# Feed-forward gate and up with the weight blocks held in TensorE and x streamed, so that the gated products come out turned

## The chip, the cores and the metric

The kernel runs on one core of one Trainium2 chip. A core has TensorE (matmuls; PE in the profile, its loads of the stationary operand PEld), VectorE (DVE), ScalarE (ACT), GpSimd (POOL), SyncE (SP, which issues the weight transfers here) and 16 DMA engines. The metric is device microseconds of one execution, less is better. Three runs of the kernel before gave 1437.35 us as their median (1436.28 to 1438.09).

## The reference

x has 256 tokens of width 1024, float32. Two attention blocks come first, then four feed-forward parts with a short convolution and a gated delta rule between them. Only the feed-forward part is changed:

```
def rms_norm_2(x, g):
    xf = x.astype(jnp.float32)
    y = xf * lax.rsqrt(jnp.mean(xf * xf, axis=-1, keepdims=True) + RMS_EPS)
    return (y * g.astype(jnp.float32)).astype(x.dtype)

def swiglu(x, w_gate_up, w_down):
    gate, up = jnp.split(x @ w_gate_up, 2, axis=-1)
    return (jax.nn.silu(gate) * up) @ w_down

        ff = swiglu(rms_norm_2(h, g[0]), ffn_w_gate_up[i, 0], ffn_w_down[i, 0])
        h = h + 0.5 * rms_norm_2(ff, g[1])
```

w_gate_up is 1024 x 5632, w_down 2816 x 1024. In each of the two layers swiglu runs before and after the mixer: four times in all.

## The kernel before, in words

Every large matmul is made of three: each operand is kept as a rounded part and the rest (`x_hi`, `x_lo`, `w_hi`, `w_lo`, all float32r), and hi*hi, hi*lo and lo*hi are summed in PSUM. Weights come in units of 2048 columns per partition (1 MB) through a ring of 4 buffers: SP issues two transfers into `raw`, ACT rounds (`split_hi`, L209), DVE forms the rest (`split_lo`, L227), TensorE uses the unit (`Walk.unit`) and counts it in `unit_used`, which frees the buffer for the load of four units later. `w_hi` and `w_lo` start a unit every 8192 bytes of a partition; `x_hi` and `x_lo` hold eight blocks of 256 columns (1024 bytes each).

A feed-forward part has 11 steps (j = 0 to 10) of 256 hidden columns. A step takes two gate-and-up units (`gate_up(j, 0)` and `gate_up(j, 1)`, each half of the 1024 input rows; 256 gate and 256 up columns side by side) and one down unit (`down`). TensorE works through them in an order written out in `Ffn.pe`: gate-up of step j, then down of step j-1, then `turn(j)`. In a unit TensorE holds a 128x128 block of x (tokens across) and streams 512 weight columns: 24 matmuls. So gate and up come out with tokens across the partitions. The banks of PSUM alternate by step: A for step 0, then G for odd and M for even ones; down sums in the four A banks.

After the second gate-up unit of a step DVE scales by the token's `r` (the norm's reciprocal root, one number per partition here) and clamps (`clamp`, L704), ACT forms the sigmoid in three operations (`sigmoid`, L669 to L671), DVE makes the product `h` (`gate`, L711 and L713), TensorE turns it with four 128x128 transposes (`turn`, L623) into the PSUM bank that gate and up have left, ACT rounds that into `hT_hi` (`hid_hi`, L677), DVE forms `hT_lo` (`hid_lo`, L722), and the down unit takes both as its held operand. The last two down units run interleaved in `last_units`.

Besides these, `Walk.turned_unit` (L280 to L282) is used by the delta-rule part alone: it holds 32-column blocks of weights and streams x's 256 columns. Units of the attention blocks that carry the chunk "gr" stream 272 columns.

Each engine runs its instructions in the order of the code (`Ffn.pe`, `Ffn.dve`, `Ffn.act`, `Ffn.sp`), with semaphores between them.

Of the kernel before, what the change touches and what calls it, by code (L numbers as in the profile page):

```python
# [172 lines left out]
class Walk:  # L173
# [112 lines left out]

    def first_units(self, pre, banks):
# [264 lines left out]
class Ffn:  # L552


    def __init__(self, net, name, w_gu, w_dn, pre_g, post_row, before, brow_free):
# [8 lines left out]
        self.h_turned = net.shared_sem("ffn_h_turned", self.steps)  # L564
# [42 lines left out]
    def turn_bank(self, j):  # L607
        return self.net.M[0] if j == 0 else self.banks(j)[0]
# [8 lines left out]
    def turn(self, w, j):  # L617
        net, pe = self.net, w.eng
        pe.wait_ge(*self.hidden(j + 1))
        bank = self.turn_bank(j)  # L620
        for kk in range(2):
            for tt in range(TT):
                mm = pe.transpose(bank[:, kk * T + tt * P:kk * T + (tt + 1) * P],  # L623
# [8 lines left out]
    def pe(self, w):  # L632
# [40 lines left out]
    def hid_hi(self, w, j):  # L673
        act = w.eng
        act.wait_ge(*self.h_turned(j + 1))
        at = 2 * (j % 2)
        act.activation(self.hT_hi[:, at:at + 2, :], self.turn_bank(j)[:, :], ACT.Copy).then_inc(self.h_hi.sem, 1)  # L677

    def act(self, w):
# [9 lines left out]
        for j in range(1, self.steps):  # L689
            w.split_hi()  # L690
            self.hid_hi(w, j - 1)
# [4 lines left out]
        self.hid_hi(w, self.steps - 1)  # L696
        self.post.act(w)


    def clamp(self, w, j):  # L700
        net, dve = self.net, w.eng
        dve.wait_ge(net.unit_used, self.unit_end["g", j, 1])
        for tt in range(TT):
            ins = dve.tensor_scalar(self.z[:, tt, :], self.banks(j)[tt][:, 0:256], net.r[:, tt:tt + 1], CLAMP,  # L704
                                    ALU.mult, ALU.max)
        ins.then_inc(self.clamped.sem, 1)

# [2361 lines left out]
```

## Time and profile before

| | |
|---|---|
| median of 3 runs | 1437.35 us |
| the profiled execution | 1436.43 us, its span 1434.7 us |
| mean granted clock of TensorE | 0.998 of full speed |
| TensorE matmuls busy | 1412.5 us (98%) |
| weight loads busy | 1159.0 us (81%) |
| VectorE, ScalarE, GpSimd busy | 999.7, 836.4, 67.8 us |
| read from HBM | 235.07 MB, 165 GB/s over the span |

The profiled execution took 1436.43 us of device time, of which the span from the first to the last instruction is 1434.7 us. Matmuls are pipelined: the duration that a row shows is that from start to end of one, and the next one starts long before that end, so the pace of a stretch is read from the starts of its first and last row, not from durations.

### The profile page before, as it was taken

The numbers are of one execution on the slowest core, as the hardware profiler recorded it, in microseconds if no ns is written. First come the engines' busy times: TensorE is split into PE (matmuls) and PEld (weight loads), VectorE is DVE, ScalarE is ACT, GpSimd is POOL, SyncE is SP. The second block draws the span as 40 slices with busy tenths as digits, with TensorE's granted clock in tenths as the row PEclk, the third lists the DMA queues.
The fourth block names the chain that finished last, engine by engine and source line by source line (L and its number), as shares of the span: only waits on it lengthen the run. The fifth ranks groups of instructions, "written<-read, shape, count | busy, mean of one in ns | idle before, by whom it ended". The sixth has DMA issues, their size and how long they took to land.

```text
span 1434.7 us, 20210 instructions
## 1 busy us (share of the span) xinstructions
PE 1412.5 (98%) x8003; PEld 1159.0 (81%) x8003; DVE 999.7 (70%) x1381; ACT 836.4 (58%) x1250; POOL 67.8 (5%) x163
## 2 busy tenths in 40 slices
PE   7999999999999999999999999999999999999998
PEld 6888888888888787788887888887778888788886
DVE  5878788876555766665557656667989876865555
ACT  6657574745454554554445555457888886554444
POOL 8000000000000000000000000001030300000000
PEclk9999999999999999999999999999999999999999
DMA  7543453345556555555655555555453432566562
GB/s 231 166 138 94 158 178 125 110 148 189 192 177 199 180 191 177 172 195 177 192 189 176 192 195 185 181 171 179 142 162 108 119 121 99 175 193 194 177 198 95
DMA packets 168286, 238.24 MB, mean 166 GB/s; under 512 B 21554, under 2 KB 114640, under 8 KB 168192
## 3 DMA queue, kind: packets, MB, share of 16 engines
q1 hardware_dynamic: 166496, 233.57, 50.2%
q0 software_dynamic: 1632, 3.35, 0.8%
q8 instruction: 64, 1.05, 0.3%
q14 instruction: 30, 0.25, 0.1%
q10 hardware_dynamic: 64, 0.02, 0.0%
HBM read 235.07 MB, written 1.84 MB: 165 GB/s over the span
## 4 chain that ended last, share of the span: by engine, by line
PE 93%; DVE 3%; ACT 2%; DMA 1%; issue 1%; SPq 0%; DVEq 0%; ACTq 0%
PE A L245 17%; PE A L246 16%; PE A L247 16%; PE M L245 5%; PE G L245 5%; PE M L247 5%; PE G L247 5%; PE G L246 5%; PE M L246 5%; PE A L1282 1%; PE G L1203 1%; PE G L1250 1%; DMA raw<-in_ffn_w_gate_up 1%; PE M L623 1%; DVE tmp L414 1%; PE M L1260 1%
## 5 line engine op out<-in xcount | busy, mean ns | idle before, releaser
L227 DVE TENSOR_TENSOR w_lo<-raw,w_hi 128x1024 fp32r<-128x1024 f32 (+2 forms) x296 | 506.1, 1731 | 167.8 <-ACT w_hi L209 167.2
L209 ACT ACTIVATE w_hi<-raw 128x1024 fp32r<-128x1024 f32 (+2 forms) x296 | 426.9, 1462 | 161.2 <-DMA raw<-in_ffn_w_gate_up 132.7
L245 PE MATMUL A<-w_hi,x_hi 128*128 128x512 f32 (+1 forms) x640 | 259.3, 405 | 3.6 <-DVE x_lo L419 0.7
L247 PE MATMUL A<-w_hi,x_lo 128*128 128x512 f32 (+1 forms) x640 | 247.5, 387 | 0.0
L246 PE MATMUL A<-w_lo,x_hi 128*128 128x512 f32 (+1 forms) x640 | 247.0, 386 | 0.0
L245 PEld LDWEIGHTS A<-w_hi,x_hi 128*128 128x128 f32 x640 | 120.7, 189 | 33.7 <-DVE x_lo L419 6.6
L247 PEld LDWEIGHTS A<-w_hi,x_lo 128*128 128x128 f32 x640 | 120.4, 188 | 25.3
L245 PE MATMUL A<-w_hi,ffn_ffn_hT_hi 128*128 128x512 f32 x352 | 138.7, 394 | 0.0
L669 ACT ACTIVATE ffn_ffn_e<-ffn_ffn_z 128x512 f32<-128x512 f32 x44 | 27.8, 632 | 190.2 <-DVE ffn_ffn_z L704 190.2
L246 PE MATMUL A<-w_lo,ffn_ffn_hT_hi 128*128 128x512 f32 x352 | 138.4, 393 | 0.0
L246 PEld LDWEIGHTS A<-w_lo,x_hi 128*128 128x128 f32 x640 | 120.9, 189 | 21.0 <-issue 0.7
L247 PE MATMUL A<-w_hi,ffn_ffn_hT_lo 128*128 128x512 f32 x352 | 137.2, 390 | 0.0
L245 PE MATMUL M<-w_hi,x_hi 128*128 128x512 f32 x320 | 126.6, 396 | 0.0
L245 PE MATMUL G<-w_hi,x_hi 128*128 128x512 f32 x320 | 126.5, 395 | 0.0
L247 PE MATMUL M<-w_hi,x_lo 128*128 128x512 f32 x320 | 124.8, 390 | 0.0
L247 PE MATMUL G<-w_hi,x_lo 128*128 128x512 f32 x320 | 124.8, 390 | 0.0
L246 PE MATMUL G<-w_lo,x_hi 128*128 128x512 f32 x320 | 124.6, 389 | 0.0
L246 PE MATMUL M<-w_lo,x_hi 128*128 128x512 f32 x320 | 124.5, 389 | 0.0
L711 DVE TENSOR_TENSOR ffn_ffn_gs<-ffn_ffn_z,ffn_ffn_e 128x512 f32<-128x512 f32 x44 | 30.4, 692 | 81.0 <-ACT ffn_ffn_e L671 81.0
L247 PEld LDWEIGHTS A<-w_hi,ffn_ffn_hT_lo 128*128 128x128 f32 x352 | 66.1, 188 | 14.9
L245 PEld LDWEIGHTS A<-w_hi,ffn_ffn_hT_hi 128*128 128x128 f32 x352 | 66.1, 188 | 14.7
L246 PEld LDWEIGHTS A<-w_lo,ffn_ffn_hT_hi 128*128 128x128 f32 x352 | 66.2, 188 | 13.1
(388 smaller groups left out, 2033.0 us busy)
## 6 DMA issues: line engine op xcount, KB each, us to landing
raw<-in_ffn_w_gate_up SPq DMA_DIRECT2D x176, 512.0 KB, 4.8
raw<-in_ffn_w_down SPq DMA_DIRECT2D x88, 512.0 KB, 4.2
raw<-in_w_in SPq DMA_DIRECT2D x48, 512.0 KB, 4.4
raw<-in_gdn_w_in SPq DMA_DIRECT2D x48, 512.0 KB, 4.6
raw<-in_sc_w_in SPq DMA_DIRECT2D x24, 512.0 KB, 4.7
raw<-in_w_out SPq DMA_DIRECT2D x16, 512.0 KB, 4.3
raw<-in_gdn_w_out SPq DMA_DIRECT2D x16, 512.0 KB, 4.1
raw<-in_w_mem_kv SPq DMA_DIRECT2D x8, 512.0 KB, 5.8
```

What stands on the lines that cost most here:

```text
L209: ins = act.activation(net.w_hi[:, v % RING, part], net.raw[:, v % RING, part], ACT.Copy)
L227: ins = dve.tensor_tensor(net.w_lo[:, v % RING, part], net.raw[:, v % RING, part], net.w_hi[:, v % RING, part].bitcast(F32), ALU.subtract)
L245: pe.matmul(out, xh, hi[:, k, c, :], start=start and k == 0, stop=False)
L246: pe.matmul(out, xh, lo[:, k, c, :], start=False, stop=False)
L247: mm = pe.matmul(out, xl, hi[:, k, c, :], start=False, stop=stop and k == nk - 1)
L414: dve.tensor_tensor(self.y(n), self.banks[n][:, :].rearrange("p (k t) -> p k t", k=4), self.g[:, 4 * h:4 * h + 4].unsqueeze(2).to_broadcas ...
L623: mm = pe.transpose(bank[:, kk * T + tt * P:kk * T + (tt + 1) * P], self.h[:, tt, kk * P:(kk + 1) * P], net.ident[:, :])
L669: w.chain(act.activation(self.e[:, :, :], self.z[:, :, :], ACT.Exp, scale=-1.0))
L711: w.chain(dve.tensor_tensor(self.gs[:, :, :], self.z[:, :, :], self.e[:, :, :], ALU.mult))
L1203: mm = pe.matmul(bank[:, n * P + t * 64:n * P + (t + 1) * 64], self.KE[rows, 1 + lev, tok], right, start=True, stop=True, tile_position=(D ...
L1250: mm = pe.matmul(bank[:, at:at + keys], qT[rows, pair, tt * P:(tt + 1) * P], kT[rows, pair, 0:keys], start=True, stop=True, tile_position= ...
L1260: mm = pe.transpose(bank[:, b * P:(b + 1) * P], self.Pb[:, i % 3, b * P:(b + 1) * P], ident[:, :])
```

## The change

Steps 1 to 10 of each feed-forward part form gate and up the other way round: the new `turned_blocks` holds a 128x128 block of weights and streams the 256 columns of x, so a unit is four column blocks times four row blocks times three: 48 matmuls of 256 columns in place of 24 of 512. The first bank gets the gate's two blocks, the second the up's. They come out turned, hidden columns across the partitions, as the down unit wants them. The transposes of steps 1 to 10 are gone, `hid_hi` and `hid_lo` read `h` in SBUF, and TensorE waits for `hidden` of step j-2 before it writes that step's banks. Step 0 stays as it was.

Since tokens now lie along the free dimension, r must be a row repeated on all partitions: DVE spreads each token's r over 128 columns (`r_cols`), two matmuls against the identity turn it, and ACT copies it to `rT` once in each part. `clamp` and `gate` become five DVE operations over 512 elements instead of five over 256 or 512.

```
+    def turned_blocks(self, x_hi, x_lo, k0, nk, banks, start, stop):
+
+        net, u, pe = self.net, self.u, self.eng
+        n = nk * 4 * P
...
+        hi = net.w_hi[:, u % RING, 0:n].rearrange("p (k n) -> p k n", k=nk)
+        lo = net.w_lo[:, u % RING, 0:n].rearrange("p (k n) -> p k n", k=nk)
+        pe.wait_ge(net.w_lo_ready, u + 1)
+        for c in range(4):
+            out, cols = banks[c // 2][:, c % 2 * T:(c % 2 + 1) * T], slice(c * P, (c + 1) * P)
+            for k in range(nk):
+                pe.matmul(out, hi[:, k, cols], x_hi[:, k0 + k, :], start=start and c % 2 == 0 and k == 0, stop=False)
+                pe.matmul(out, hi[:, k, cols], x_lo[:, k0 + k, :], start=False, stop=False)
+                mm = pe.matmul(out, lo[:, k, cols], x_hi[:, k0 + k, :], start=False,
+                               stop=stop and c % 2 == 1 and k == nk - 1)
+        mm.then_inc(net.unit_used, 1)
+        self.u += 1
...
     def gate_up(self, w, j, kh):
         net = self.net
-        if kh == 0 and j >= 2:
-            w.eng.wait_ge(*self.h_lo(j - 1))
-        b0, b1 = self.banks(j)
-        w.unit(net.x_hi, net.x_lo, 4 * kh, 4, 512, [[b0], [b1]], kh == 0, kh == 1)
+        if kh == 0 and j == 2:
+            w.eng.wait_ge(*self.h_lo(1))
+            w.eng.wait_ge(*self.rT_ready(1))
+        elif kh == 0 and j > 2:
+            w.eng.wait_ge(*self.hidden(j - 1))
+        w.turned_blocks(net.x_hi, net.x_lo, 4 * kh, 4, self.banks(j), kh == 0, kh == 1)
+
+    def turn(self, w):
         net, pe = self.net, w.eng
-        pe.wait_ge(*self.hidden(j + 1))
-        bank = self.turn_bank(j)
+        pe.wait_ge(*self.r_spread(1))
+        for tt in range(TT):
+            mm = pe.matmul(net.M[1][:, tt * P:(tt + 1) * P], self.r_cols[:, tt, :], net.ident[:, :],
+                           start=True, stop=True)
+        mm.then_inc(self.r_rows.sem, 1)
+        pe.wait_ge(*self.hidden(1))
...
         self.gate_up(w, 1, 0)
-        self.turn(w, 0)
+        self.turn(w)
         self.gate_up(w, 1, 1)
         self.down(w, 0)
-        self.turn(w, 1)
         last = self.steps - 1
         for j in range(2, last):
             self.gate_up(w, j, 0)
             self.gate_up(w, j, 1)
             if j < last - 1:
                 self.down(w, j - 1)
-                self.turn(w, j)
         self.gate_up(w, last, 0)
-        self.turn(w, last - 1)
         self.gate_up(w, last, 1)
         self.down(w, last - 2)
-        self.turn(w, last)
...
+    def clamp(self, w, j):
+        net, dve = self.net, w.eng
+        r = self.rT[:, :].unsqueeze(1).to_broadcast([P, 2, T])
+        gate, up = (bank[:, :].rearrange("p (k t) -> p k t", k=2) for bank in self.banks(j))
+        if j == 1:
+            dve.wait_ge(*self.rT_ready(1))
+        dve.wait_ge(net.unit_used, self.unit_end["g", j, 1])
+        w.chain(dve.tensor_tensor(self.z[:, :, :], gate, r, ALU.mult))
+        dve.tensor_scalar(self.z[:, :, :], self.z[:, :, :], CLAMP, None, ALU.max).then_inc(self.clamped.sem, 1)
+        w.chain.mark(dve.tensor_tensor(self.gs[:, :, :], up, r, ALU.mult))
+
+    def gate(self, w, j):
+        dve = w.eng
+        w.chain.sync()
+        dve.wait_ge(*self.clamped(j + 1))
+        w.chain(dve.tensor_tensor(self.gs[:, :, :], self.gs[:, :, :], self.z[:, :, :], ALU.mult))
+        dve.wait_ge(*self.gated(j + 1))
+        dve.tensor_tensor(self.h[:, :, :], self.gs[:, :, :], self.e[:, :, :], ALU.mult)\
+           .then_inc(self.hidden.sem, 1)
```

On TensorE, at the border between the down unit of step 0 and the gate-up of step 2 of the first feed-forward part, before the change (a row's last field is the streamed columns as partitions x columns; `h` is the product to be turned):

```order
L246 MATMUL A<-w_lo,ffn_ffn_hT_hi 128x512
L247 MATMUL A<-w_hi,ffn_ffn_hT_lo 128x512
L623 MATMUL G<-ident,ffn_ffn_h 128x128 x4
L245 MATMUL M<-w_hi,x_hi 128x512
L246 MATMUL M<-w_lo,x_hi 128x512
```

Such a group of four transposes stood behind every down unit but the last ones; the gate-up behind it now follows directly. What is left of it in the changed kernel is this one place in each part, between the two gate-up units of step 1, with the two new matmuls that turn r ahead of it:

```order
L300 MATMUL G<-x_hi,w_lo 128x256
L643 MATMUL M<-ident,ffn_ffn_r_cols 128x128 x2
L649 MATMUL M<-ident,ffn_ffn_h 128x128 x4
L298 MATMUL G<-x_hi,w_hi 128x256
L299 MATMUL G<-x_lo,w_hi 128x256
L300 MATMUL G<-x_hi,w_lo 128x256
```

On DVE a middle step before the change, from its clamp to that of the next step (L227 are the rests of weight units):

```order
L704 TENSOR_SCALAR ffn_ffn_z<-M,small 128x256 x2
L711 TENSOR_TENSOR ffn_ffn_gs<-ffn_ffn_z,ffn_ffn_e 128x512
L713 SCALAR_TENSOR_TENSOR ffn_ffn_h<-M,small,ffn_ffn_gs 128x256 x2
L227 TENSOR_TENSOR w_lo<-raw,w_hi 128x2048 x2
L722 TENSOR_TENSOR ffn_ffn_hT_lo<-M,ffn_ffn_hT_hi 128x512
L227 TENSOR_TENSOR w_lo<-raw,w_hi 128x2048
```

and the same stretch now:

```order
L759 TENSOR_TENSOR ffn_ffn_z<-M,ffn_ffn_rT 128x512
L760 TENSOR_SCALAR ffn_ffn_z<-ffn_ffn_z 128x512
L761 TENSOR_TENSOR ffn_ffn_gs<-M,ffn_ffn_rT 128x512
L767 TENSOR_TENSOR ffn_ffn_gs<-ffn_ffn_gs,ffn_ffn_z 128x512
L769 TENSOR_TENSOR ffn_ffn_h<-ffn_ffn_gs,ffn_ffn_e 128x512
L227 TENSOR_TENSOR w_lo<-raw,w_hi 128x2048
L776 TENSOR_TENSOR ffn_ffn_hT_lo<-ffn_ffn_h,ffn_ffn_hT_hi 128x512
L227 TENSOR_TENSOR w_lo<-raw,w_hi 128x2048 x2
```

Here `hT_lo` is formed one weight unit earlier than before, and out of SBUF.

## Rows read from the trace of the kernel before

**Rows 1.** The page: busy time of engines, clock, share of the last-ending chain.

```profile
PE 1412.5 (98%) x8003; PEld 1159.0 (81%) x8003; DVE 999.7 (70%) x1381; ACT 836.4 (58%) x1250; POOL 67.8 (5%) x163
...
PEclk9999999999999999999999999999999999999999
...
PE 93%; DVE 3%; ACT 2%; DMA 1%; issue 1%; SPq 0%; DVEq 0%; ACTq 0%
```

**Rows 2.** Waits of PE, the longest: us in total, times, longest.

```profile
PE M L3046 <- DMA rows<-in_g_pre: 7.4, 1, 7.4
```

**Rows 3.** Timeline of PE, step 2 of the first part: start, us, what.

```profile
372.25 0.60 PE L623 MATMUL G<-ident,ffn_ffn_h 128*128 128x128 f32 x4
372.60 0.48 PE L245 MATMUL M<-w_hi,x_hi 128*128 128x512 f32 x1
...
378.18 0.39 PE L245 MATMUL M<-w_hi,x_hi 128*128 128x512 f32 x1
...
383.62 0.39 PE L245 MATMUL A<-w_hi,ffn_ffn_hT_hi 128*128 128x512 f32 x1
...
389.12 0.60 PE L623 MATMUL M<-ident,ffn_ffn_h 128*128 128x128 f32 x4
389.48 0.48 PE L245 MATMUL G<-w_hi,x_hi 128*128 128x512 f32 x1
```

**Rows 4.** Timeline of PE, 32 weight columns held, x's 256 streamed.

```profile
987.01 0.28 PE L280 MATMUL A<-x_hi,w_hi 128*32 128x256 f32 x1
...
988.60 0.28 PE L282 MATMUL A<-x_lo,w_hi 128*32 128x256 f32 x1
```

**Rows 5.** Timeline of PE, 128x128 blocks of x held, 272 columns streamed.

```profile
178.00 0.29 PE L245 MATMUL A<-w_hi,x_hi 128*128 128x272 f32 x1
...
181.03 0.40 PE L245 MATMUL A<-w_hi,x_hi 128*128 128x512 f32 x1
```

**Rows 6.** Timeline of PE, eight plain float32 matmuls of 128 columns.

```profile
1146.42 1.05 PE L2478 MATMUL M<-gdn_gd_S,gdn_gd_MT 128*128 128x128 f32 x8
```

**Rows 7.** Weight loads by form: shape, count, busy us, mean ns.

```profile
L245 PEld LDWEIGHTS G<-w_hi,x_hi 128*128 128x128 f32 x320 | 60.1, 188 | 11.9
...
L280 PEld LDWEIGHTS A<-x_hi,w_hi 128*32 128x32 f32 x8 | 0.9, 108 | 1.2 <-ACT gdn_gd_u L2514 1.2
```

**Rows 8.** Groups by form, DVE and ACT: busy us, mean ns, idle before.

```profile
L227 DVE TENSOR_TENSOR w_lo<-raw,w_hi 128x2048 fp32r<-128x2048 f32 x145 | 329.5, 2290 | 149.0 <-ACT w_hi L209 148.9
L711 DVE TENSOR_TENSOR ffn_ffn_gs<-ffn_ffn_z,ffn_ffn_e 128x512 f32<-128x512 f32 x44 | 30.4, 692 | 81.0 <-ACT ffn_ffn_e L671 81.0
L414 DVE TENSOR_TENSOR tmp<-G,cols 128x512 f32<-128x512 f32 x16 | 10.6, 689 | 3.0 <-PE G L361 2.6
L2755 DVE TENSOR_SCALAR gdn_gd_sg<-gdn_gd_t 128x512 f32<-128x512 f32 x16 | 6.7, 427 | 0.1
```

**Rows 9.** Busy time by engine in that step, clock, DMA share, GB/s.

```profile
372.60:389.48 16.88, 16.88 (x80) 13.92 (x78) 9.84 (x10) 7.87 (x8) 0.00 (x0) 1.00 0.59 187
```

**Rows 10.** Timeline of DVE in that step: a weight unit, then the clamp.

```profile
380.85 2.29 DVE L227 TENSOR_TENSOR w_lo<-raw,w_hi 128x2048 fp32r<-128x2048 f32 x1 [4.11 <-ACT w_hi L209]
383.81 0.88 DVE L704 TENSOR_SCALAR ffn_ffn_z<-M,small 128x256 f32<-128x256 f32 x2 [0.67 <-PE M L247]
```

**Rows 11.** Timeline of DVE and PE at the last step of that part.

```profile
479.56 0.88 DVE L704 TENSOR_SCALAR ffn_ffn_z<-M,small 128x256 f32<-128x256 f32 x2 [1.58 <-PE M L247]
...
484.27 2.29 DVE L227 TENSOR_TENSOR w_lo<-raw,w_hi 128x2048 fp32r<-128x2048 f32 x1 [0.20 <-ACT w_hi L209]
486.48 0.68 DVE L722 TENSOR_TENSOR ffn_ffn_hT_lo<-M,ffn_ffn_hT_hi 128x512 fp32r<-128x512 f32 x1
...
485.22 0.48 PE L245 MATMUL A<-w_hi,ffn_ffn_hT_hi 128*128 128x512 f32 x1
```

**Rows 12.** Timeline of DVE and PE around step 0's turn.

```profile
325.60 0.88 DVE L713 SCALAR_TENSOR_TENSOR ffn_ffn_h<-A,small,ffn_ffn_gs 128x256 f32<-128x256 f32 x2
...
327.07 0.60 PE L623 MATMUL M<-ident,ffn_ffn_h 128*128 128x128 f32 x4
```

More of the change, by code:

```diff
@@ L285, in turned_unit @@
             self.u += 1
+    def turned_blocks(self, x_hi, x_lo, k0, nk, banks, start, stop):
+        net, u, pe = self.net, self.u, self.eng
+        n = nk * 4 * P
+        assert net.sizes[u] == n, (u, net.sizes[u], n)
+        hi = net.w_hi[:, u % RING, 0:n].rearrange("p (k n) -> p k n", k=nk)
[10 more added lines that the diff above has]
+        self.u += 1
     def first_units(self, pre, banks):
@@ L563, in __init__ @@
         self.hidden = net.shared_sem("ffn_hidden", self.steps)
-        self.h_turned = net.shared_sem("ffn_h_turned", self.steps)
+        self.h_turned = net.shared_sem("ffn_h_turned", 1)
+        self.r_spread = net.shared_sem("ffn_r_spread", 1)
+        self.r_rows = net.shared_sem("ffn_r_rows", 1)
+        self.rT_ready = net.shared_sem("ffn_rT", 1)
         self.h_hi = net.shared_sem("ffn_h_hi", self.steps)
@@ L582, in tensors @@
         self.h = net.sb("ffn_h", [P, TT, 256])
+        self.r_cols = net.sb("ffn_r_cols", [P, TT, P])
+        self.rT = net.sb("ffn_rT", [P, T])
         self.hT_hi = net.sb("ffn_hT_hi", [P, 4, T], F32R)
@@ L673, in hid_hi @@
     def hid_hi(self, w, j):
[L674 to L677, printed above, removed]
+        act, at = w.eng, 2 * (j % 2)
+        if j == 0:
+            act.wait_ge(*self.h_turned(1))
+            src = self.net.M[0][:, :]
+        else:
+            act.wait_ge(*self.hidden(j + 1))
+            src = self.h[:, :, :]
+        if j >= 2:
+            act.wait_ge(self.net.unit_used, self.unit_end["d", j - 2])
+        act.activation(self.hT_hi[:, at:at + 2, :], src, ACT.Copy).then_inc(self.h_hi.sem, 1)
     def act(self, w):
@@ L690, in act @@
             w.split_hi()
-            self.hid_hi(w, j - 1)
+            if j == 1:
+                act.wait_ge(*self.r_rows(1))
+                act.activation(self.rT[:, :], self.net.M[1][:, 0:T], ACT.Copy).then_inc(self.rT_ready.sem, 1)
+                self.hid_hi(w, 0)
             if j < self.steps - 1:
@@ L695, in act, with first_clamp, first_gate @@
             w.split_hi()
-        self.hid_hi(w, self.steps - 1)
+            self.hid_hi(w, j)
         self.post.act(w)
-    def clamp(self, w, j):
+    def first_clamp(self, w):
         net, dve = self.net, w.eng
-        dve.wait_ge(net.unit_used, self.unit_end["g", j, 1])
+        dve.wait_ge(net.unit_used, self.unit_end["g", 0, 1])
         for tt in range(TT):
-            ins = dve.tensor_scalar(self.z[:, tt, :], self.banks(j)[tt][:, 0:256], net.r[:, tt:tt + 1], CLAMP,
+            ins = dve.tensor_scalar(self.z[:, tt, :], self.banks(0)[tt][:, 0:256], net.r[:, tt:tt + 1], CLAMP,
                                     ALU.mult, ALU.max)
         ins.then_inc(self.clamped.sem, 1)
-    def gate(self, w, j):
+        for tt in range(TT):
+            ins = dve.tensor_scalar(self.r_cols[:, tt, :], net.ident[:, :], 0.0, net.r[:, tt:tt + 1],
+                                    ALU.mult, ALU.add)
+        ins.then_inc(self.r_spread.sem, 1)
+    def first_gate(self, w):
         net, dve = self.net, w.eng
-        dve.wait_ge(*self.gated(j + 1))
+        dve.wait_ge(*self.gated(1))
         w.chain(dve.tensor_tensor(self.gs[:, :, :], self.z[:, :, :], self.e[:, :, :], ALU.mult))
         for tt in range(TT):
-            ins = dve.scalar_tensor_tensor(out=self.h[:, tt, :], in0=self.banks(j)[tt][:, 256:512],
+            ins = dve.scalar_tensor_tensor(out=self.h[:, tt, :], in0=self.banks(0)[tt][:, 256:512],
                                            scalar=net.r[:, tt:tt + 1], in1=self.gs[:, tt, :],
@@ L734, in dve @@
         dve.wait_ge(*self.pre.r_ready(1))
-        self.clamp(w, 0)
+        self.first_clamp(w)
         w.split_lo()
-        self.gate(w, 0)
+        self.first_gate(w)
         for j in range(1, self.steps):
             w.split_lo()
-            self.hid_lo(w, j - 1)
+            if j == 1:
+                self.hid_lo(w, 0)
             if j < self.steps - 1:
@@ L745, in dve @@
             w.split_lo()
-        self.hid_lo(w, self.steps - 1)
+            self.hid_lo(w, j)
         self.post.dve(w)
```

12 lines of the change are left out of this document (5 added, 7 removed).

## The prediction

> **What bounds the kernel now.** I read the page first. TensorE's matmuls are busy 98% of the span, the chain that ended last lies on PE for 93% of it, and the clock's row shows 0.9 or more of full speed in all 40 slices [rows 1]; the step I use below has 1.00 [rows 9], the upper of the two levels, 2.4 GHz. Next the waits: the longest that PE has is 7.4 us at the program's start [rows 2], and none of any feed-forward part is among them. DVE is busy 9.84 us and ACT 7.87 us of a 16.88 us step, the DMA engines 0.59 of it [rows 9]. So the time is the sum of what TensorE issues, and a change is worth what it takes from or adds to that row of starts. The reader should see that busy shares and durations can't tell it: a 512-column matmul shows 0.39 to 0.48 us, yet 24 of them start within 5.44 us. Only starts give the price.
>
> **A step in starts.** In step 2 [rows 3] the second gate-up unit runs from 378.18 to 383.62: 5.44 us for 24 matmuls, 226.7 ns each. The first one, right behind the transposes, runs from 372.60 to 378.18: 5.58 us, 0.14 more for the same work, so a group of transposes also costs a slow restart. The down unit takes 5.50 us (383.62 to 389.12), and the transposes 0.36 us (389.12 to 389.48). 5.58 + 5.44 + 5.50 + 0.36 = 16.88 us.
>
> **Removed.** Ten groups of four transposes in each of four parts. Each is 0.36 us, and the restart behind it 0.14 us: 40 x 0.50 = 20.0 us, all of it on TensorE's row. The transposes waited for `hidden` and had no idle time in front of them, so no more than that is saved. The restart I count whole, since the border between two kinds of fp32r units without transposes between them, 383.62, shows none: the down unit is 5.50 us and the gate-up in front of it 5.44.
>
> **The price of a pair.** This term decides. A gate-up unit was 24 pairs (load of the held block, matmul) of 512 columns and becomes 48 of 256; there are 80 such units, 3840 new pairs. So each nanosecond by which a pair is over or under half of 226.7, which is 113.4, is worth 3.84 us. No row shows this very pair. The nearest:
> - The same streamed operand, x's 256 columns, with blocks of 32 weight columns held, summed into one place of a bank as here: from 987.01 to 988.60 are 14 pairs, 1.59 us, 113.6 ns each [rows 4]. This is again half of the 512-column pace within the rounding, so streaming costs in proportion to columns and no fixed cost per matmul shows.
> - What differs there is the load: 32 columns, 108 ns, against 188 ns for 128 [rows 7]. The difference, 80 ns for 96 columns, is 0.83 ns a column, so that 128 columns should occupy the load path for about 107 ns, an estimate. Eight float32 matmuls of 128 columns with full 128-column loads take 1.05 us with the last one's whole length of about 0.27; the seven gaps are 0.78 us, 111 ns each [rows 6]. A full load fits into 111 ns, then, and 113.4 is more, by 2 ns. This is thin.
> - Blocks of x held, 272 columns streamed: 24 pairs from 178.00 to 181.03, 3.03 us, 126.2 ns each [rows 5]. In proportion 272 columns would be 120.4, so these pay 5.8 ns each. Less 16 columns, that would be 119.5 at 256.
>
> The first and second say 113.4, the third 119.5. I take 113.4. The third row's weight blocks start every 272 columns, 1088 bytes; those of the new code, held and streamed, all start at multiples of 512 bytes from their tiles' starts, as the operands of the gate-up before do, which runs at 226.7 with no such extra. That the starts are the reason is a guess, and the range keeps both ends.
>
> The Trainium skill's page "TensorE: Matmul & The Clock Gate", section "LDWEIGHTS (loading the stationary operand)", has a load take its columns over 1.2 GHz, 107 ns for 128; the trace agrees in its slope [rows 7]. Its section "Back-to-back issue gap" gives a matmul of N columns N/2.4 + 2.5 ns: 109.2 for 256, by which the sum would be 16 us lower than mine. The trace contradicts it at both widths, 226.7 against 215.8 and 113.6 against 109.2.
>
> With 113.4, the 80 units cost 48 x 113.4 = 5.44 us as before: 0.
>
> **Added on TensorE.** Eight matmuls that turn r, two per part, 0.11 us each by the 111 ns gap [rows 6]: 0.9 us. They wait for `r_spread`, formed on DVE right after step 0's clamp, a whole weight unit ahead of the turn. Behind them the remaining turn waits for step 0's `hidden`. It is done at 326.48 and used at 327.07 [rows 12]; the two spreads ahead of it on DVE, 128 columns each and so under 0.43 us each [rows 8], add at most 0.7 with their start, while the turn itself starts 0.2 later for the r matmuls. Cost 0 to 0.1 us a part.
>
> **DVE and ACT.** In a middle step DVE did two scale-and-clamps, one product, two fused products and the rest. Now it has four two-operand products and one rest over 512 elements, 0.69 us each [rows 8], and a clamp of 0.43: 3.9 us, with three weight units of 2.29 us [rows 8] 10.8 us of a step of 16.4. It was 9.84 [rows 9]. That is hidden below 5.6 us of slack, and the wait it sits on has moved: `hT_lo` was needed by a transpose chain and is now needed by the down unit that follows 10.9 us of gate-up. ACT's work is the same but for one copy in a part. If the cover were gone, the 1 us a step would cost 40 us; it would need another 5 us of DVE work.
>
> A place where the slack is small is the last step of a part [rows 11]. `hT_lo` ends at 487.16; `last_units` needs it 12 matmuls, 2.77 us, behind 485.22, at 487.99. The new kernel's TensorE is there 0.5 us sooner (487.49), and the clamp's two dependent operations, 0.69 + 0.43 with a semaphore's way between, take 0.3 longer than the 0.88 before, which delays sigmoid, weight unit and `hT_lo` to 487.46. I count 0.1 us for each part, 0 to 0.4: 0.4 us in all.
>
> The weight stream: a step reads 3 MB at 187 GB/s [rows 9]; 0.5 us less makes it 192. The DVE half of a weight unit ends at 383.14, when the clamp's matmuls end near 383.6 [rows 10], and TensorE wants that unit only after the down unit and the transposes, at 389.48. 6.3 us of slack; losing 0.5 costs nothing.
>
> **Sum**, against the profiled execution's 1436.4: -20.0 + 0 + 0.9 + 0.1 + 0.4 = -18.6, 1417.8 us. The median of the runs shown is 0.9 higher, so 1418.7 against it.
>
> **Rivals.**
> 1. Forecast: the pair costs 112 to 114.5 ns: 1413 to 1423 us. Chance 0.62.
> 2. In between, 114.5 to 117.4 ns: the load, 2 ns short of being the bound, slips out in part. 1423 to 1434 us, 0.12.
> 3. The other side: a 128-column load that runs beside the whole of a short stream disturbs it as in [rows 5], 5.8 ns a pair or more. At 119.5 ns the extra is 6.1 x 3.84 = 23.4 us, 1442 us: slower by 0.3%. Should a pair cost 126.2, it would be 1468. It decides from 118.9 ns on, where 21 us have gone. For it: 272-column pairs have 9 ns more room over the load than the new ones, and yet pay. Against it: [rows 4] and the 512-column units pay nothing. Chance 0.21, of which 0.05 lies within 0.2% of before.
> 4. The page's 109.2 ns: 1403 us; against it stand both paces above. 0.03.
> 5. TensorE's saving is eaten by another wait, the weight stream or DVE's chain ahead of the down unit: steps stay near 16.9 us, 1437 us. Only with 5 us of slack gone on every step; DMA engines busy 0.59. 0.02.
>
> **The numbers.** A measurement of this kernel tells about 0.2%, 2.9 us, from no change. Faster: cases 1, 2 and 4, 0.76 with a little of 2 taken off. Within 0.2%: 0.08, from 3, 5 and the edge of 2. Slower 0.16, all from case 3. The range, 1413.5 to 1438, holds 1, 2, 5 and the near edge of 3; its low end is a pair of 112 ns, the load's own pace.
>
> **What would show it.** In the changed trace, a gate-up unit of 48 starts within 5.44 us (5.74 means rival 3, 5.24 rival 4); a step from clamp to clamp of 16.4 us; no slow restart behind a down unit; loads still 188 ns long; no wait of PE for `h` or `hT_lo` over 0.4 us; 160 fewer transposes. The forecast is wrong if the pair isn't 113.4 ns, and by 3.84 us for each nanosecond; anything else here is under 2 us.

## The result, and the profile after

| | median us | lowest to highest | runs |
|---|---|---|---|
| before | 1437.12 | 1436.28 to 1438.09 | 5 |
| after | 1444.04 | 1441.67 to 1445.86 | 5 |

The ratio is 1.0045 (1.0033 to 1.0057): the change makes the kernel 0.45% slower, 6.9 us. The forecast was 1418.7. The profiled execution took 1441.67 us.

The page of the changed kernel, the rows that answer to [rows 1]:

```profile
PE 1418.3 (99%) x9779; PEld 1243.1 (86%) x9779; DVE 1027.4 (71%) x1389; ACT 835.7 (58%) x1254; POOL 67.9 (5%) x163
...
PEclk9999999999999999999999999999999999999999
...
PE 93%; DVE 2%; ACT 2%; DMA 2%; issue 1%; SPq 0%; DVEq 0%; ACTq 0%
```

The clock is as before, and TensorE is still the chain. Its longest wait is still the one at the start, and no matmul of a feed-forward step stands in the list, neither for `h` nor for `hT_lo`:

```profile
PE M L3099 <- DMA rows<-in_g_pre: 6.7, 1, 6.7
```

So the loss must lie in TensorE's own pace. Step 2 in starts, from the timeline of PE, against [rows 3]:

```profile
370.50 0.28 PE L298 MATMUL M<-x_hi,w_hi 128*128 128x256 f32 x1
...
382.02 0.40 PE L245 MATMUL A<-w_hi,ffn_ffn_hT_hi 128*128 128x512 f32 x1
...
387.53 0.28 PE L298 MATMUL G<-x_hi,w_hi 128*128 128x256 f32 x1
```

A pair is one load of a held block with its matmul. The two gate-up units, 96 pairs, take 382.02 - 370.50 = 11.52 us, 120.0 ns a pair; the down unit 5.51. The step is 17.03 us where it was 16.88 and the forecast had 16.4. The next one is 16.99, so a step costs 0.13 us more on average, 5 us in forty.

Step 0 of that part, where r is turned ahead of `hidden`:

```profile
324.36 0.60 PE L643 MATMUL M<-ident,ffn_ffn_r_cols 128*128 128x128 f32 x4
324.80 0.60 PE L649 MATMUL M<-ident,ffn_ffn_h 128*128 128x128 f32 x4
325.16 0.36 PE L298 MATMUL G<-x_hi,w_hi 128*128 128x256 f32 x1
```

The two r matmuls show as four rows (x4) and take 0.44 us; 1.8 us over four parts.

The step by windows (busy time of PE, PEld, DVE, ACT, POOL, then clock, DMA share and GB/s), against [rows 9], and two loads of a whole block by form, against [rows 7]:

```profile
370.50:387.53 17.03, 17.03 (x122) 16.03 (x120) 10.52 (x10) 7.97 (x8) 0.00 (x0) 1.00 0.56 186
```

```profile
L299 PEld LDWEIGHTS G<-x_lo,w_hi 128*128 128x128 f32 x640 | 122.6, 192 | 0.9
L298 PEld LDWEIGHTS M<-x_hi,w_hi 128*128 128x128 f32 x640 | 121.1, 189 | 0.7
```

DVE has 10.52 us, 0.3 under the estimate; clock and memory traffic are those of before; a load is about as long as it was, 189 to 192 ns against 188. At the last step of the part:

```profile
485.98 0.68 DVE L776 TENSOR_TENSOR ffn_ffn_hT_lo<-ffn_ffn_h,ffn_ffn_hT_hi 128x512 fp32r<-128x512 f32 x1
...
486.83 0.46 PE L245 MATMUL A<-w_hi,ffn_ffn_hT_hi 128*128 128x512 f32 x1
```

`hT_lo` ends at 486.66, just ahead of its matmul; the slip there is under 0.1 us.

### The profile page after: what moved, and what is told of

It reads as the page before. It is cut to its first block, busy times and chain, and to the rows that moved or that the text cites. A ratio compares the mean times of both kernels' runs of the same rounds, so it can differ in the third digit from the quotient of the medians.

```text
span 1439.9 us, 23894 instructions
## 1 busy us (share of the span) xinstructions
PE 1418.3 (99%) x9779; PEld 1243.1 (86%) x9779; DVE 1027.4 (71%) x1389; ACT 835.7 (58%) x1254; POOL 67.9 (5%) x163
## 4 chain that ended last, share of the span: by engine, by line
PE 93%; DVE 2%; ACT 2%; DMA 2%; issue 1%; SPq 0%; DVEq 0%; ACTq 0%
PE A L245 17%; PE A L247 16%; PE A L246 16%; PE M L298 5%; PE M L299 5%; PE M L300 5%; PE G L300 5%; PE G L298 5%; PE G L299 5%; PE A L1335 1%; PE G L1256 1%; PE G L1303 1%; DMA raw<-in_ffn_w_gate_up 1%; DVE tmp L432 1%; PE M L1313 1%
## 5 line engine op out<-in xcount | busy, mean ns | idle before, releaser
L227 DVE TENSOR_TENSOR w_lo<-raw,w_hi 128x1024 fp32r<-128x1024 f32 (+2 forms) x296 | 508.2, 1730 | 190.0 <-ACT w_hi L209 189.0
L298 PE MATMUL M<-x_hi,w_hi 128*128 128x256 f32 x640 | 181.2, 283 | 0.0
L298 PE MATMUL G<-x_hi,w_hi 128*128 128x256 f32 x640 | 181.2, 283 | 0.0
L299 PE MATMUL M<-x_lo,w_hi 128*128 128x256 f32 x640 | 181.2, 283 | 0.0
L300 PE MATMUL M<-x_hi,w_lo 128*128 128x256 f32 x640 | 181.2, 283 | 0.0
L300 PE MATMUL G<-x_hi,w_lo 128*128 128x256 f32 x640 | 181.0, 283 | 0.0
L299 PE MATMUL G<-x_lo,w_hi 128*128 128x256 f32 x640 | 180.9, 283 | 0.0
L299 PEld LDWEIGHTS G<-x_lo,w_hi 128*128 128x128 f32 x640 | 122.6, 192 | 0.9
L298 PEld LDWEIGHTS G<-x_hi,w_hi 128*128 128x128 f32 x640 | 122.6, 192 | 0.8
L300 PEld LDWEIGHTS G<-x_hi,w_lo 128*128 128x128 f32 x640 | 122.6, 192 | 0.0
L298 PEld LDWEIGHTS M<-x_hi,w_hi 128*128 128x128 f32 x640 | 121.1, 189 | 0.7
```

Source lines behind the costliest of these rows:

```text
L227: ins = dve.tensor_tensor(net.w_lo[:, v % RING, part], net.raw[:, v % RING, part], net.w_hi[:, v % RING, part].bitcast(F32), ALU.subtract)
L298: pe.matmul(out, hi[:, k, cols], x_hi[:, k0 + k, :], start=start and c % 2 == 0 and k == 0, stop=False)
L299: pe.matmul(out, hi[:, k, cols], x_lo[:, k0 + k, :], start=False, stop=False)
L300: mm = pe.matmul(out, lo[:, k, cols], x_hi[:, k0 + k, :], start=False, stop=stop and c % 2 == 1 and k == nk - 1)
```

## The experiments

Three theories stood at the outset. A pair costs 120.0 because **the load is the bound** in a short pair; because each float32r (fp32r) matmul has a **fixed cost** (at one column in each cycle of 2.4 GHz, 256 columns are 106.7 ns, 13.3 less than 120.0; 512 are 213.3, 13.4 less than 226.7); or because load and stream **disturb each other**. The later runs ask by what. A time of one execution has no interval, the others have. Some kernels leave products incomplete; they are there for the pace only.

**turnsback.** The changed kernel with the forty groups of transposes put back, their result unused.

```diff
+    def turn_idle(self, w, j):
+        pe = w.eng
+        pe.wait_ge(*self.hidden(j + 1))
+        bank = self.banks(j)[0]
+        for kk in range(2):
+            for tt in range(TT):
+                pe.transpose(bank[:, kk * T + tt * P:kk * T + (tt + 1) * P],
+                             self.h[:, tt, kk * P:(kk + 1) * P], self.net.ident[:, :])
...
                 self.down(w, j - 1)
+                self.turn_idle(w, j)
```

> The changed kernel with the four transposes of steps 1 to 10 put back behind the same down units, their result thrown away (they wait for h and write into a bank that nobody reads until it is overwritten). Theory (the removed part was priced right at 0.36 us plus 0.14 us of slow restart, 0.50 us a time, 40 times): 20 us more than the changed kernel. Rival (the transposes cost only their own 0.36 us, since the restart is slow in some other way with 256-column pairs): 14.4 us more, the unit behind the transposes as long as the others.

```profile
373.84 0.60 PE L645 MATMUL G<-ident,ffn_ffn_h 128*128 128x128 f32 x4
374.20 0.36 PE L298 MATMUL M<-x_hi,w_hi 128*128 128x256 f32 x1
...
385.79 0.39 PE L245 MATMUL A<-w_hi,ffn_ffn_hT_hi 128*128 128x512 f32 x1
```

1461.11 us, ratio 1.0166 (1.0145 to 1.0186), about 17 us over the changed kernel, between the 14.4 and the 20 expected. A group is 0.36 us, and the gate-up behind it 11.59, 0.08 over the 11.51 mean of a step without it: 0.44 x 40 = 17.6. What the change removes is real, then; the loss is made elsewhere.

**split256.** The kernel before, x's blocks held, but each gate-up stream of 512 cut into two of 256.

```diff
+            if halves:
+                for n, (a, b) in enumerate(((0, 256), (256, 512))):
+                    pe.matmul(out[:, a:b], xh, hi[:, k, c, a:b], start=start and k == 0 and n == 0, stop=False)
...
+                continue
             pe.matmul(out, xh, hi[:, k, c, :], start=start and k == 0, stop=False)
```

> The kernel before, with every 512-column matmul of the gate-up of steps 1 to 10 cut in two of 256 on the same held block of x, so that the same products are formed by 3840 more pairs; transposes as before. Theory F (a pair of a 128-column float32r load and a matmul of N columns takes N/2.4 + 13.3 ns): 120.0 ns a pair, 5.76 us a unit, about 25 us more than the kernel before (1462 us in its profiled execution). Theory L (the load alone takes 120 ns, streams cost in proportion to columns): 120 ns too. Rival R (the extra cost comes from weights being held and x streamed, or from where they lie): 113.4 ns a pair and 1437 us.

```profile
371.29 0.48 PE L247 MATMUL M<-w_hi,x_hi 128*128 128x256 f32 x2
...
382.88 0.39 PE L254 MATMUL A<-w_hi,ffn_ffn_hT_hi 128*128 128x512 f32 x1
```

1457.14 us in one execution. 96 pairs in 11.59 us, 120.7 with the slow restart behind the transposes in it. So it is not the swap of operands: 256-column pairs are dear in either role.

**held64, held112, stream128.** The changed kernel with smaller pairs in 10 or 11 of 12: 64 or 112 weight columns held, or 128 tokens streamed.

```diff
-                pe.matmul(out, hi[:, k, cols], x_lo[:, k0 + k, :], ...)
+                some = slice(c * P, c * P + 64)      # held112: 112
+                pe.matmul(out[0:64], hi[:, k, some], x_lo[:, k0 + k, :], ...)
```

```diff
+                pe.matmul(out[:, 0:128], hi[:, k, cols], x_lo[:, k0 + k, 0:128], ...)   # stream128
```

> The changed kernel with only the first 64 of each 128 held weight columns used in 10 of 12 matmuls, so that half of the gate and up products are left incomplete; streams of 256 columns as before. Theory L (load-bound pairs): a load of half the columns is far from the bound, and pairs fall to 113.4 ns. Theory F (a fixed cost a pair, 13.3 ns with 128 held columns and 6.7 with 32): between the two, about 115.6 ns if it grows evenly with held columns. Rival I (a load that runs beside the stream disturbs it, and half the load disturbs half as long): about 116.7 ns.

```profile
369.87 0.28 PE L302 MATMUL M<-x_lo,w_hi 128*64 128x256 f32 x1
...
370.89 0.28 PE L302 MATMUL M<-x_lo,w_hi 128*64 128x256 f32 x1
```

Nine pairs in 1.02 us, 113.3 ns: in this kernel half a load beside 256 columns takes the extra away. Where whole blocks stand between them (2 of 12), the 96 pairs of a step take 11.03 us, 114.9 each. 1424.12 us in one execution. The load-bound theory had told 113.4; the next run decides about it.

> The changed kernel with only the first 128 tokens streamed in 11 of 12 matmuls (half of the products are left incomplete); loads of 128 columns as before. Theory L (a float32r load of 128 columns takes 120 ns whatever is streamed): pairs stay at 120 ns. Theory F (13.3 ns on top of the stream, the load hidden as long as it fits): the stream of 53 + 13 ns is far shorter than the load, and the pair falls to the load's own pace, about 111 ns as with the eight plain float32 matmuls.

```profile
368.78 0.28 PE L299 MATMUL M<-x_hi,w_hi 128*128 128x128 f32 x1
...
369.78 0.33 PE L299 MATMUL M<-x_hi,w_hi 128*128 128x256 f32 x1
```

Nine pairs in 1.00 us, 111 ns, with whole loads. A load that can follow a load every 111 ns is no bound of 120, and that theory falls. 1413.98 us in one execution.

> The changed kernel with 112 of each 128 held weight columns used in 10 of 12 matmuls (part of the products is left incomplete), streams of 256. Theory P: a load of 112 columns beside the stream takes 112/128 of 120, or 105 ns, less than the stream's 113.4, so pairs fall to 113.4. Theory F with a part that grows from 64 to 128 columns: about 118 ns.

```profile
372.58 0.28 PE L299 MATMUL M<-x_hi,w_hi 128*128 128x256 f32 x1
...
383.94 0.40 PE L245 MATMUL A<-w_hi,ffn_ffn_hT_hi 128*128 128x512 f32 x1
```

11.36 us for 96, 118.3 ns (11.30 us in every other step, 117.7), 1436.59 us in one execution: in between. At 256 columns the extra grows with the held columns above 64. A fixed cost per matmul would not: 113.3 with 64 held rules it out as the whole story.

**bstream384, bheld64, bheld64b.** The kernel before with 384 of 512 columns streamed in 10 of 12, and with 64 of 128 tokens held in 10 of 12, or nearly all.

```diff
-            pe.matmul(out, xh, lo[:, k, c, :], start=False, stop=False)
+            pe.matmul(out[:, 0:384], xh, lo[:, k, c, 0:384], ...)          # bstream384
+            pe.matmul(out[0:64, :], xh[:, 0:64], lo[:, k, c, :], ...)     # bheld64, bheld64b
```

> The kernel before, with 384 instead of 512 columns streamed in 10 of 12 matmuls of the gate-up of steps 1 to 10 (part of the products is left incomplete), 128 tokens held. Theory P: 170.0 ns a pair. Theory F: 160 + 13.3 = 173.3 ns.

```profile
364.90 0.34 PE L248 MATMUL M<-w_lo,x_hi 128*128 128x384 f32 x1
...
366.46 0.33 PE L248 MATMUL M<-w_lo,x_hi 128*128 128x384 f32 x1
```

Nine pairs in 1.56 us, 173.3 ns. 120.0, 173.3 and 226.7 lie 53.3 ns apart for 128 columns each, one column in a cycle of 2.4 GHz. With whole blocks held at these places the pace is thus columns over 2.4 GHz plus 13.3 ns at all three widths: the 226.7 from which I took a half had that constant in it once, and two halves have it twice.

> The kernel before, with only 64 of each 128 tokens of x held in 10 of 12 matmuls of the gate-up of steps 1 to 10 (half of the products are left incomplete), streams of 512 weight columns. Theory P (streaming costs 17/16 of N/2.4, and a pair is the longer of this and of a load that is slowed by a stream running beside it): 226.7 ns a pair, no gain. Theory F (a pair is N/2.4 plus a fixed part that goes with the held columns, 6.7 ns up to 64 and 13.3 for 128): 220.0 ns.

> The kernel before, with 64 of 128 tokens held in all but the first and last matmuls of an accumulation (half of the products are left incomplete), streams of 512: long unmixed rows of half loads, which the earlier run with mixed shapes didn't give. Theory F (N/2.4 plus a part that goes with the held columns): 220.0 ns. Theory P (with half loads the stream's cost is 17/16 of N/2.4): 226.7 ns.

The second, from its timeline of PE:

```profile
372.95 0.48 PE L247 MATMUL M<-w_hi,x_hi 128*128 128x512 f32 x1
...
384.07 0.39 PE L247 MATMUL A<-w_hi,ffn_ffn_hT_hi 128*128 128x512 f32 x1
```

11.12 us for 48, 231.7 ns, where the same stretch with whole blocks took 11.02, 229.6 ns [rows 3] (both with the slow restart behind the transposes), and 1440.7 us for each of the two kernels in one execution: slower than with whole blocks. Neither theory had that, and it stays open. That half a load takes the extra away is seen at 256 columns only.

**hpad, hpad_after, allpad.** Was the place in memory the reason? By the sizes of the tensors, one behind the other as the kernels allocate them, the weight tensors and x's two parts start at the same place modulo 1024 bytes, and `hT_hi` 704 bytes behind it. From here on "n bytes off" is this distance from the weights' place. A pad of 320 bytes takes `hT_hi` to it, and `hT_lo`, 4096 bytes behind, with it. hpad does it to the kernel before, hpad_after to the changed one, allpad also to the memory and convolution operands.

```diff
+        net.sb("ffn_pad", [P, 80])        # 320 bytes a partition
         self.hT_hi = net.sb("ffn_hT_hi", [P, 4, T], F32R)
```

> The kernel before, with 320 unused bytes a partition in front of hT_hi, so that hT_hi and hT_lo start at the same multiple of 1024 bytes as x_hi and the weight units do. Theory A (the down unit's 229.1 ns a pair against 226.7 of gate-up come from where its held blocks lie against the streamed ones): the 44 down units fall from 5.50 to 5.44 us, 2.4 us less than before in all (ratio 0.9983). Rival (they come from the PSUM banks changing every six matmuls): no change.

```profile
367.15 0.39 PE L245 MATMUL A<-w_hi,ffn_ffn_hT_hi 128*128 128x512 f32 x1
...
372.60 0.60 PE L624 MATMUL G<-ident,ffn_ffn_h 128*128 128x128 f32 x4
```

The down unit takes 5.45 us, 227.1 ns a pair, where it took 5.50 [rows 3]; 1434.18 us, ratio 0.9982 (0.9971 to 0.9992). No instruction was changed, so the place of the held operand has a price: 2.1 ns a pair.

> The changed kernel with the 320 unused bytes in front of hT_hi that made the down unit of the kernel before faster. If the two are independent: the down unit falls from 5.50 to 5.45 us, 2.3 us less than the changed kernel, about 1441.5 us, still slower than before by 0.3%.

1443.50 us, 1.0041 (1.0028 to 1.0055), gate-up still 11.51 to 11.52 us a step: `hT_hi`'s place alone does not move the 120. The down unit takes 5.46.

> The kernel before with hT_hi, the memory operands mem_hi and the short convolution's y_hi all moved to the same multiple of 1024 bytes as x_hi and the weight units. Theory A: the down units as in the run with hT_hi alone (2.4 us), the memory operands' 234 ns pairs and the convolution's 229 ns pairs fall to 227, another 192 x 7 + 192 x 6 + 96 x 2.3 ns, 2.7 us: 5 us less than before, ratio 0.9965. Rival: only hT gives anything, 0.9982.

A memory unit in allpad, whose 11 pairs from the second on took 2.56 us before:

```profile
296.11 0.39 PE L246 MATMUL A<-w_lo,block_mem_hi 128*128 128x512 f32 x1
...
298.63 0.39 PE L245 MATMUL A<-w_hi,x_hi 128*128 128x512 f32 x1
```

2.52 us here, 229.1 ns instead of 232.7. In the total it does not show beyond hpad: 1434.08 us, 0.9981 (0.9968 to 0.9994), where 0.9965 was expected.

**xpad, xpad_timed.** The changed kernel with x moved by 704 bytes, and `hT` with it. The second is the same kernel, timed.

```diff
+        self.sb("x_pad", [P, 176])        # 704 bytes a partition
         self.x_hi = self.sb("x_hi", [P, KT, T], F32R)
```

> The changed kernel with 704 unused bytes a partition in front of x_hi and x_lo, so that the streamed blocks start at other multiples within 1024 bytes than the held weight blocks. Theory A (where held and streamed blocks start against each other matters for short pairs too): a pair of 256 costs more than 120.0, 2 to 6 ns. Rival (120.0 is the fixed cost alone, and starts matter only to some shapes): 120.0 as it was. In units where x is held and 512 weight columns are streamed, theory A gives 229 ns in place of 226.7.

> The changed kernel with x_hi and x_lo moved by 704 bytes, the same kernel as the look that gave 1430.6 us, now timed. Theory E (the rhythm is fixed by the program, by what each stretch enters with): about 1430 us in every run, ratio 0.9955 to the kernel before. Rival (it is chance from run to run): a median between 1430 and 1446 with a wide spread.

From xpad_timed, the timeline of PE:

```profile
367.12 0.39 PE L246 MATMUL A<-w_hi,ffn_ffn_hT_hi 128*128 128x512 f32 x1
...
372.69 0.28 PE L299 MATMUL M<-x_hi,w_hi 128*128 128x256 f32 x1
...
383.58 0.39 PE L246 MATMUL A<-w_hi,ffn_ffn_hT_hi 128*128 128x512 f32 x1
```

Gate-up takes 10.89 us, 113.4 ns a pair: the forecast's price, with whole loads and the same instructions. The down unit, whose held tensor is now 384 bytes off, pays 5.57 us. 1425.26 us (1423.67 to 1426.57, 6 runs), ratio 0.9920 (0.9906 to 0.9935). xpad had the same pace by step 2, against both of its expectations, and 1430.55 us in one execution, from which the second expectation took its 1430. Three of its feed-forward parts are as long as here (169.9 to 170.1 us in both). The difference lies between the third part and the fourth, 290.8 us against 286.0: there TensorE stood still for 1.4 us twice, and from 1068 to 1072 us its granted clock was 0.57.

The two executions of this one kernel also differ in pace elsewhere. The stretch of [rows 4], 32 weight columns held, whose 14 pairs took 1.59 us in the kernel before, from the timelines of PE in xpad and then in xpad_timed:

```profile
979.76 0.28 PE L281 MATMUL A<-x_hi,w_hi 128*32 128x256 f32 x1
...
981.44 0.28 PE L283 MATMUL A<-x_lo,w_hi 128*32 128x256 f32 x1
```

```profile
979.18 0.28 PE L281 MATMUL A<-x_hi,w_hi 128*32 128x256 f32 x1
...
980.77 0.28 PE L283 MATMUL A<-x_lo,w_hi 128*32 128x256 f32 x1
```

That is 1.68 and 1.59 us, 120.0 and 113.6 ns a pair, at clock 1.00 and with the DMA engines busy throughout in both. The first unit of the first part takes 5.65 us in xpad and 5.46 in xpad_timed, 117.7 and 113.8 ns. So the same instructions at the same addresses can run at two paces, from one execution to the next; and a light load is no guarantee of the fast one. In kernels with x and the weights where the kernel before has them, the same 14 pairs take 113.6 (before, held64), 115.0 (bheld64, stream128) or 115.7 ns (after, turnsback, bstream384).

**bx704, ax704.** x 704 bytes off and `hT` brought to the weights' place, in both kernels, so that operands are swapped at equal placement.

```diff
+        self.sb("x_pad", [P, 176])
         self.x_hi = self.sb("x_hi", [P, KT, T], F32R)
...
+        net.sb("ffn_pad", [P, 160])
         self.hT_hi = net.sb("ffn_hT_hi", [P, 4, T], F32R)
```

> The kernel before with x_hi and x_lo moved by 704 bytes and hT_hi padded so that it starts where the weight units do (modulo 1024). Theory A (place of held against streamed blocks): the pairs that hold x and stream 512 columns cost 229.3 instead of 226.7 ns, down units 5.45 us; 3840 pairs of x more by 2.6 ns, 10 us, and the x units of the other parts by 1 to 2 ns, less 2.4 us for hT: about 1447 us. Rival (the distance matters to 256-column pairs alone): 1435.

```profile
371.25 0.48 PE L246 MATMUL M<-w_hi,x_hi 128*128 128x512 f32 x1
...
382.34 0.39 PE L246 MATMUL A<-w_hi,ffn_ffn_hT_hi 128*128 128x512 f32 x1
```

11.09 us against 11.02 [rows 3]: 512-column pairs lose 1.5 ns by this move, where 2.6 were expected. 1439.58 us, 1.0020 (1.0011 to 1.0029).

> The changed kernel with x moved by 704 bytes, as in the look that gave 1430.6, and hT_hi padded back to the weight units' place. Theory A: 256-column pairs 113.4 ns, down units 5.45 us instead of 5.58 (44 of them, 5.7 us): about 1425 us, ratio 0.992 to the kernel before. Rival (the look was a chance of that run, or the pad of hT_hi moves something else): 1430 or more.

```profile
320.72 0.28 PE L299 MATMUL G<-x_hi,w_hi 128*128 128x256 f32 x1
...
326.18 0.38 PE L645 MATMUL M<-ident,ffn_ffn_r_cols 128*128 128x128 f32 x2
...
371.47 0.28 PE L299 MATMUL M<-x_hi,w_hi 128*128 128x256 f32 x1
...
382.77 0.39 PE L246 MATMUL A<-w_hi,ffn_ffn_hT_hi 128*128 128x512 f32 x1
...
388.21 0.28 PE L299 MATMUL G<-x_hi,w_hi 128*128 128x256 f32 x1
```

A miss, and a telling one. The first unit of the part runs 48 pairs in 5.46 us, 113.8 ns. In step 2 the same kind of pair, at the same placement (modulo 1024), takes 11.30 us for 96, 117.7 ns, behind a down unit of 5.44. It is so in all four parts: the two units of step 1, which no down unit precedes, run fast (the second takes 5.54 with its restart), and every one from step 2 on runs at 117.7 to 117.8, also the last step, which follows a gate-up directly. There are two paces at one placement, and here what ran ahead seems to pick. 1435.06 us, 0.9983 (0.9974 to 0.9992).

**ax64, ax256.** As ax704, x 64 and 256 bytes off.

```diff
+        self.sb("x_pad", [P, 16])         # ax256: 64
...
+        net.sb("ffn_pad", [P, 64])        # ax256: 16
```

> As ax704, with x moved by 64 bytes only. If the load and the stream, which start together, meet in the same piece of memory only when they lie at nearly the same place: 113.4 ns already. If only a large distance frees them: near 120.

```profile
357.81 0.28 PE L299 MATMUL G<-x_hi,w_hi 128*128 128x256 f32 x1
...
369.12 0.40 PE L246 MATMUL A<-w_hi,ffn_ffn_hT_hi 128*128 128x512 f32 x1
```

> As ax704, with x moved by 256 bytes. If the conflict goes by the distance within 512 bytes (704 is 192 there) and grows smoothly: 113 to 117 ns. If what frees the pair is the distance alone being other than 0: 113.4. Units that hold x and stream 512: 229 to 234.

```profile
355.39 0.28 PE L299 MATMUL G<-x_hi,w_hi 128*128 128x256 f32 x1
...
366.91 0.40 PE L246 MATMUL A<-w_hi,ffn_ffn_hT_hi 128*128 128x512 f32 x1
```

11.31 us (117.8 ns) and 11.52 us (120.0 ns); 1442.23 and 1442.89 us in one execution each. Neither is what its expectation had. The first unit of a part, ahead of any down unit, gives the same order without that influence: 5.75 us in the changed kernel and in ax256, 5.65 in ax64, 5.46 in ax704.

**axh320.** x 704 bytes off, and `hT` too: both now sit where `hT` sat in the kernel before.

```diff
+        self.sb("x_pad", [P, 176])
...
+        net.sb("ffn_pad", [P, 80])
```

> As xpad_timed, with hT_hi and hT_lo moved by another 320 bytes, so that they start where x does (modulo 1024). Theory E: the down unit's own pairs change to the 226, 229, 232 ns pattern of x (5.50 us), and the gate-up stretches behind it run at 113.4 or at 117.8 ns, all alike; 1427 us or 1444 us. Rival (hT_hi's place can't reach the gate-up pairs, and ax704 was slow for another reason): 113.4 ns and 1427 us.

```profile
369.80 0.28 PE L299 MATMUL M<-x_hi,w_hi 128*128 128x256 f32 x1
...
380.70 0.39 PE L246 MATMUL A<-w_hi,ffn_ffn_hT_hi 128*128 128x512 f32 x1
...
386.20 0.28 PE L299 MATMUL G<-x_hi,w_hi 128*128 128x256 f32 x1
```

Gate-up 10.90 us, 113.5 ns; down 5.50; a step of 16.40, which is the step the prediction named. The down unit's place does reach the gate-up pairs, then: ax704 differs from this kernel in nothing else. **1421.63 us** (1419.44 to 1423.89, 5 runs), ratio 0.9895 (0.9880 to 0.9910): 1.0% faster than the kernel before and about 1.5% faster than the changed one. Against the kernel before at the best placement tried for it (hpad), the swapped order is about 0.9% faster.

The placements side by side (bytes off the weights, modulo 1024; x for the pairs of 256, the held operand for those of 512):

| off | pair of 256 columns, ns | pair of 512 columns, ns | from |
|---|---|---|---|
| 0 | 120.0 | 226.7 | after, [rows 3], hpad |
| 64 | 117.8 | | ax64 |
| 256 | 120.0 | | ax256 |
| 384 | | 232.1 (down, 5.57 / 24) | xpad_timed |
| 704 | 113.4 with `hT` 384 or 704 off, 117.7 with `hT` at 0 | 229.2 (down, 5.50 / 24) | xpad_timed, axh320, ax704, [rows 3] |

## Why the prediction was wrong

**The step that failed** is the price of a pair: "With 113.4, the 80 units cost 48 x 113.4 = 5.44 us as before: 0." A pair costs 120.0. That is 6.6 ns over, 6.6 x 3.84 = 25.3 us. With it the sum is -20.0 + 25.3 + 1.8 for r = +7.1 us; the medians differ by 6.9 and the two profiled executions by 5.2. The three parts whose end the timelines show are 1.9, 2.2 and 2.4 us longer than before (the first 175.26 against 173.37), where the sum gives 1.8 for each; the rest, 0.1 to 0.6 us, is small beside the step that failed. The profiled executions differ by less because that of the kernel before came to the first part 3.0 us later, part of it in a stretch at a lower clock (0.66 from 224 to 229 us).

Within that step two things went wrong. First, half of 226.7 was read as a price per column. bstream384 shows a constant in it at these places: 226.7 is 213.3 + 13.4, and a short pair pays 13.3 again. What seemed to deny a constant, [rows 4], had 32 columns held; in held64 half a load at 256 columns brings the pair to 113.3. So the row that agreed with the half may have done so for a reason of its own, the load's width, and that was the very item in which it differed. And it agreed partly by luck: the same 14 pairs show 115.7 in the changed kernel's trace, and up to 120.0 in xpad's. One row of one execution was no firm price. Second, the extra of [rows 5] was set aside because the new blocks "all start at multiples of 512 bytes from their tiles' starts, as the operands of the gate-up before do, which runs at 226.7 with no such extra". Starts do matter, as guessed, but the equal starts are no guard against the extra: beside 256 columns they are among the dear ones, 120.0, as 256 bytes off is too, and 704 bytes off the pair costs 113.4 (xpad_timed, axh320). For 512 columns the equal starts are the cheap ones, 226.7 against 228 to 232. So the constant belongs to the placement as well: at 704 bytes off it is 6.7 ns at 256 columns and, by the 1.5 ns of bx704, about 15 at 512.

**Point by point.**
- What bounds the kernel: right. TensorE's starts, clock level and waits are as read.
- Removed, 20.0 us: right by the starts of the kernel before. Put back into the changed kernel the groups cost 17 us, since the restart there is 0.08 and not 0.14.
- The load fits into 111 ns: right (stream128). That it "slips out in part" is not what costs: the load's own pace allows 111.
- r, 0.9 us: 1.8. A plain float32 matmul of 128 columns shows as two rows of 0.11 us, so two of them are 0.44, and I had counted one each. The eight of [rows 6] are for the same reason four matmuls; the 111 ns between two loads stand.
- Waits at the turn and at `hT_lo`, 0.5 us: none is listed, and at the place of `hT_lo` in the trace after it is under 0.1.
- DVE 10.8 us a step: 10.5, hidden as said. The weight stream: hidden, 186 GB/s.
- Rival 3 came true, with its side and very nearly its price: 119.5 ns and 1442 us told, 120.0 and 1444 measured. It had 0.21. Its one supporting row, [rows 5], was the only one of the three that showed float32r pairs with whole blocks held beside a short stream, and I set it aside by a guess on starts that no row tested. The nearness of the price is partly luck: rows 5 has its blocks at other starts, and the 119.5 rests on a placement that the new pairs don't have.
- Rival 4, 109.2 ns: no gate-up unit with 48 pairs of 256 columns took less than 5.45 us, 113.5 ns each, in any run. In the Trainium skill, "TensorE: Matmul & The Clock Gate", section "Back-to-back issue gap", the formula behind the 109.2 stands for an isolated matmul and not for a stream of pairs of load and matmul, so the prediction asked it about something else.

**What is shown and what isn't.** Shown: in the forty steps the extra is there with whole blocks held and gone with 64; it does not depend on which operand is held (split256, at equal starts); it goes away when x moves by 704 bytes with the instructions unchanged, as long as `hT` is not at the weights' place. Not shown: what in the memory or the engine is behind it. Nor whether it is the distance between the two operands or the place of one of them that counts: the weights moved in no run, and everything allocated behind x moved with it. Two paces, 113.8 and 117.7, occur at one placement, and ax704 against axh320 and xpad_timed shows the down unit's placement deciding between them. It is not the only thing that does: in xpad the first unit of the first part took 5.65 us (117.7 ns), in axh320 that of the fourth, though no down unit runs ahead of either and the other first units of these two placements take 5.45 to 5.47, and both are back at 113.4 by step 2. Within a trace the forty steps are alike, and all five executions of the changed kernel took longer than all five of the kernel before, so chance is no cause of the loss. What makes a stretch enter one pace or the other is open. So is bheld64. And the extra at the forty steps is explained by measured pairs, but the totals of ax64 and ax256 (1442 us) are so only in part: ax64's feed-forward parts are 2 us shorter than those of the changed kernel (173.0 to 173.3 against 175.3 to 175.6), and it loses that outside them (it enters the first one 4.8 us later). The 512-column units there were not priced one by one.

## What to carry to other kernels

Where a pair of load and matmul repeats thousands of times, its price may only be taken from rows with the same held width, the same streamed width and the same placement of the two operands, and from more than one stretch; a row that differs in one of them is no ground for a few per cent, however well it fits a proportion. When an operand order looks slow by a few nanoseconds a pair, move one tensor by a few hundred bytes before judging the order: here the change is worth +0.45% as it was placed and -1.05% with 1024 bytes of padding a partition. Placement also has a cost for the neighbours (down units 5.44 to 5.58 us), so the whole is timed, not the unit.

## What the runs showed of the hardware

- Where x and `hT` start moves a float32r pair by 5 to 7 ns with no instruction changed: 113.4 to 120.0 ns at 256 columns, 226.7 to 232.1 at 512, equal starts being dear at 256 and cheap at 512.
- Holding half as many columns made 256-column pairs faster (113.3 ns, held64) and 512-column pairs slower (231.7 against 229.6 in the same stretch, bheld64b).
- Whole 128-column loads follow each other every 111 ns beside fp32r matmuls of 128 columns (stream128), though each shows 191 ns in the records.
- The same instructions at the same placement have two paces, 113.8 and 117.7 ns (ax704), and which one holds depends in part on where an earlier unit's operand lies (ax704 against axh320).
- One kernel can show a stretch at 120.0 ns a pair in one execution and at 113.6 in another, at the same granted clock (32 columns held, 256 streamed; xpad and xpad_timed).
